# A two-block transformer kernel on one Trainium2 core: transposes and splits of the next linear's input inside the last chunk of the linear before

## The reference, cut to what matters

```python
# block 1
h = x + rms_norm(pool_mixer(rms_norm(x))) * post_gain      # pool_w_out: 4096 -> 2048
h = h + sigmoid(rms_norm(h) @ ple_w_gate) * (p @ ple_w_proj)
h = h + rms_norm(mla(rms_norm(h))) * post_gain              # mla_w_in, ..., mla_w_out
h = h + sigmoid(rms_norm(h) @ ple_w_gate) * (p @ ple_w_proj)
# block 2
mem_n = rms_norm(mem)
h = h + hybrid_mixer(rms_norm(h))                           # w_in: 2048 -> 6168, w_out
h = h + cross_attention(rms_norm(h), mem_n)                 # w_cq, w_ckv, w_co
h = h + conv_ffn(rms_norm(h))                               # w_up, w_down
out = rms_norm(h)
```

## Time and profile before

| what | value |
|---|---|
| median of 3 runs | 2591.68 us (2591.64 to 2591.83) |
| the profiled execution, its own time | 2595.02 us |
| its span in the trace | 2593.2 us |
| PE busy | 2519.5 us, 97% of the span |
| DVE busy | 1540.7 us, 59% |
| ACT busy | 1326.6 us, 51% |
| POOL busy | 83.7 us, 3% |
| mean granted TensorE clock | 0.995 of full speed |
| read from memory | 447.25 MB, 173 GB/s over the span |

### The profile page before, as it was taken

How to read it: one execution, slowest core, us unless ns; L and a number is a source line. 1 busy time by engine, 2 the same in 40 slices (tenths; PEclk the granted TensorE clock), 3 DMA queues, 4 the chain that set the end, 5 groups by cost and what they waited for, 6 DMA issues and landing times. The chain is left out here.

```text
span 2593.2 us, 34914 instructions
## 1 busy us (share of the span) xinstructions
PE 2519.5 (97%) x12890; PEld 2140.7 (83%) x12890; DVE 1540.7 (59%) x1814; ACT 1326.6 (51%) x1747; POOL 83.7 (3%) x124
## 2 busy tenths in 40 slices
PE   8999999999999999999899998899999999999998
PEld 7888888888778898778688887777888888888886
DVE  6665766644655555565555445755666666776554
ACT  5544444544656656464555445435544544554443
POOL 0000000000000000110100002000000000000010
PEclk9999999999999999999999999999999999999999
DMA  8666666555455543565566662054456666656563
GB/s 294 189 188 189 186 188 185 200 194 185 163 162 182 176 132 132 179 228 187 155 181 182 190 190 64 30 165 146 130 172 192 180 193 182 190 171 202 195 199 110
DMA packets 233424, 450.95 MB, mean 174 GB/s; under 512 B 14468, under 2 KB 59728, under 8 KB 232285
## 3 DMA queue, kind: packets, MB, share of 16 engines
q1 hardware_dynamic: 230518, 435.97, 54.2%
q0 software_dynamic: 2624, 13.27, 1.5%
q10 hardware_dynamic: 168, 0.19, 0.0%
HBM read 447.25 MB, written 2.12 MB: 173 GB/s over the span
## 5 line engine op out<-in xcount | busy, mean ns | idle before, releaser
L1598 DVE TENSOR_TENSOR w_lo<-raw,w_hi 128x1024 fp32r<-128x1024 f32 x852 | 1047.2, 1234 | 820.6 <-ACT w_hi L1102 801.6
L1102 ACT ACTIVATE w_hi<-raw 128x1024 fp32r<-128x1024 f32 x852 | 898.9, 1059 | 995.1 <-PE ps L648 637.0
L669 PE MATMUL ps<-x_hi_lo,w_hi 128*128 128x512 f32 x2336 | 822.9, 394 | 13.9 <-DVE w_lo L1598 13.9
L671 PE MATMUL ps<-x_hi_lo,w_lo 128*128 128x256 f32 x2336 | 661.1, 283 | 0.0
L669 PEld LDWEIGHTS ps<-x_hi_lo,w_hi 128*128 128x128 f32 x2336 | 439.4, 188 | 117.0 <-issue 8.7
L646 PE MATMUL ps<-w_hi,x_hi_lo 128*128 128x512 f32 (+3 forms) x1280 | 500.9, 391 | 21.1 <-DVE x_hi_lo L1627 12.4
L648 PE MATMUL ps<-w_hi,x_hi_lo 128*128 128x512 f32 (+3 forms) x1280 | 493.1, 385 | 0.0
L647 PE MATMUL ps<-w_lo,x_hi_lo 128*128 128x512 f32 (+3 forms) x1280 | 491.5, 384 | 0.0
L671 PEld LDWEIGHTS ps<-x_hi_lo,w_lo 128*128 128x128 f32 x2336 | 439.8, 188 | 0.0
L646 PEld LDWEIGHTS ps<-w_hi,x_hi_lo 128*128 128x128 f32 x1280 | 241.5, 189 | 76.3 <-issue 23.8
L648 PEld LDWEIGHTS ps<-w_hi,x_hi_lo 128*128 128x128 f32 x1280 | 241.2, 188 | 43.2
(11 more groups left out here) (316 smaller groups left out, 2200.4 us busy)
## 6 DMA issues: line engine op xcount, KB each, us to landing
raw<-in_w_up SPq DMA_DIRECT2D x160, 512.0 KB, 3.9
raw<-in_pool_w_in SPq DMA_DIRECT2D x128, 512.0 KB, 3.8
raw<-in_w_in SPq DMA_DIRECT2D x96, 480.0 KB, 4.0
raw<-in_w_down SPq DMA_DIRECT2D x76, 512.0 KB, 4.6
raw<-in_pool_w_out SPq DMA_DIRECT2D x64, 512.0 KB, 4.4
raw<-in_ple_w_gate SPq DMA_DIRECT2D x64, 512.0 KB, 4.0
raw<-in_mla_w_in SPq DMA_DIRECT2D x56, 448.0 KB, 3.5
raw<-in_pool_w_group SPq DMA_DIRECT2D x32, 512.0 KB, 4.3
```

What stands on the lines that cost most here:

```text
L669: pe.matmul(bank, w_hi[:, slot, cols], xs[:, k].rearrange("p s n -> p (s n)"), start=k == 0, stop=False, skip_group_check=True)
L671: last = pe.matmul(bank[:, 0:T], w_lo[:, slot, cols], xs[:, k, 0, :], start=False, stop=k == nkt - 1, skip_group_check=True)
L1102: act.activation(w_hi[:, u % RING, :], raw[:, slot, :], ACT.Copy).then_inc(S("w_hi"), 1)
L1598: dve.tensor_tensor(w_lo[:, u % RING, :], raw[:, u % RAW, :], w_hi[:, u % RING, :].bitcast(F32), ALU.subtract)\
```

## The change

PE gets `turn` and `early_turns` as functions of their own. `early` is the number of groups that a first chunk finds already done. On PE turn g of the next linear stands ahead of unit g + 1 of the last chunk in front of it, so that tile pair g of the old input has been read when group g is overwritten:

```diff
-        def first_chunk(src, source_ready=None, width=512, banks_ready=None, run=chunk):
+        def first_chunk(src, source_ready=None, width=512, banks_ready=None, run=chunk, early=0):
-            first = t.n["bank"]
+            first = t.n["bank"] - early
             def ready(k):
                 if k % 2 == 0:
-                    if k // 2 + 3 < KT // 2:
-                        turn(k // 2 + 3)
+                    if early <= k // 2 + 3 < KT // 2:
+                        turn(src, source_ready, k // 2 + 3)
                     n = first + k // 2
                     pe.wait_ge(S(f"t_free{n % 4}"), n // 4 + 2)
-            for g in range(3):
-                turn(g)
+            for g in range(early, 3):
+                turn(src, source_ready, g)
+        def early_turns(src, source_ready, n):
+            def ready(k):
+                if k % 2 == 0 and 2 <= k <= 2 * n:
+                    turn(src, source_ready, k // 2 - 1)
+            return ready
```

The two gates get 2 early groups, turned between the third and the fourth chunk of the projection; `mla_in`, `z`, `cq` get 6 in the last chunk in front of them:

```diff
-        def layer_end(n, ready_ple):
+        def layer_end(n, ready_ple, last):
+            updated = lambda g: pe.wait_ge(S(f"h_post{n}"), g // 2 + 1)
             for c in range(NCH):
                 chunk(ph, pl, 2, ready=ready_ple if c == 0 else None)
...
+                if c == 2:
...
+                    for g in range(2):
+                        turn(h, updated, g)
+            linear(h, updated, early=2, last=last)
...
-        first_chunk(h, lambda g: gated(pe, 0, g // 2 + 1), MIN_W)
+        updated0 = lambda g: gated(pe, 0, g // 2 + 1)
+        layer_end(0, ready_ple, early_turns(h, updated0, 6))
+        first_chunk(h, updated0, MIN_W, early=6)
```

For `z` the matmul of the position table (line 971), its waits and ACT's copy of it move from behind both `ckv` chunks to between them. For `up`, whose linear in front has four short chunks, two turns and groups follow each of the chunks 1 to 3 of `co`, and the `co` input moves to the last four tiles of x, which groups 6 and 7 alone overwrite:

```diff
         for c in range(NCH):
-            chunk(xh, xl, 4, ready=ready if c == 0 else None)
+            chunk(xh[:, 12:16], xl[:, 12:16], 4, ready=ready if c == 0 else None)
+            if c:
+                for g in (2 * c - 2, 2 * c - 1):
+                    turn(h, lambda g: chunk_out(pe, "co", g // 2), g)
```

ACT and DVE follow. In ACT's last chunk a group now includes its square and stands ahead of a unit; in the first chunk after it six units come ahead of group 6:

```diff
+        def early_groups(n, *args, ready=None, **kw):
+            hi(2)
+            for g in range(n):
+                if ready:
+                    ready(g)
+                group(g, *args, **kw)
+                hi(1)
+            hi(6 - n)
...
             for g in range(KT // 2):
-                if features is None:
...
+                if g >= early:
+                    if ready:
+                        ready(g)
+                    group(g, g0, src, slot, features)
                 hi(1)
```

DVE has the same without squares. Its `layer_end` splits groups 0 and 1 after the second of the three plain chunks of the projection; `update(2)` and `update(3)` stay in the gate's first chunk. For `ckv`, ACT waits before group g until PE has used unit g of the gate's last chunk (`gate1_units`); nothing is turned there. The loads of the memory move forward on POOL:

```diff
             for c in range(NCH):
                 chunk_out(pool, ("pool_out", "mla_out")[n], c)
+                if n == 1 and c == 0:
+                    load(memf, a["mem_features"], "mem_in")
+                    load(memt, tokens(a["mem_2"][0]), "mem_in")
...
-        load(memf, a["mem_features"], "mem_in")
-        load(memt, tokens(a["mem_2"][0]), "mem_in")
         gated(pool, 1)
```

More of the change, by code:

```diff
@@ L723, in first_chunk, with turn, linear @@
             run(xh, xl, KT, width, ready)
[L725 to L729, removed]
+        def turn(src, source_ready, g):
+            if source_ready:
+                source_ready(g)
+            to_bank(src, g * 256)
+        def early_turns(src, source_ready, n):
[3 more added lines that the diff above has]
+            return ready
+        def linear(src, source_ready=None, banks_ready=None, early=0, last=None):
+            first_chunk(src, source_ready, banks_ready=banks_ready, early=early)
+            for c in range(3):
+                chunk(xh, xl, KT, ready=last if c == 2 else None)
         def columns(xhi=xh, xlo=xl, nkt=KT, turns=2, ready=None, width=512):
@@ L1285, in layer_end @@
                 read_out(chunk(1), lambda tt: proj[:, tt, c * 512:(c + 1) * 512])
+                if c == 2:
+                    for g in range(2):
+                        group(g, GAIN[f"ple{n}"], h, slot + 1)
             for c in range(NCH):
-                s = first_chunk(GAIN[f"ple{n}"], h, slot + 1) if c == 0 else chunk(8)
+                s = first_chunk(GAIN[f"ple{n}"], h, slot + 1, early=2) if c == 0 else chunk(8) if c < 3 else chunk_with(next_groups)
                 act.wait_ge(S("gated"), 4 * n + c + 1)
@@ L1434, in _, with gate1_units, memory_groups @@
                 split_p(1)
[L1435 to L1440, removed]
+        def gate1_units(g):
+            products(act, "gate1", g - 7)
+        def memory_groups():
+            act.wait_ge(S("mem_in"), 32)
+            early_groups(6, GAIN["mem"], memt, 8, memf, ready=gate1_units)
+        layer_end(1, 6, memory_groups)
+        s = first_chunk(GAIN["mem"], memt, 8, features=memf, early=6, ready=gate1_units)
+        read_out(s, lambda tt: kvm[:, tt, 0:512], scale=8)
         from_bank(relrow, (slice(0, A_H), slice(0, 384)))
@@ L1631, in xpose_lo, with group, early_groups, first_chunk @@
                 t.add("xh")
-        def first_chunk(g0=None, slot=None, between=None, features=None, sem=None):
-            for g in range(KT // 2):
[L1636 to L1640, removed]
+        def group(g, g0=None, features=None, sem=None):
+            k = slice(2 * g, 2 * g + 2)
+            if features is None:
+                xpose_lo(xl[:, k, :], xh[:, k, :], 2, None if g0 is None else g0 + 2 * g)
+            else:
+                split_lo(xl, xh, features, g, g0, sem)
+        def early_groups(n, *args):
+            lo(2)
+            for g in range(n):
+                group(g, *args)
+                lo(1)
+            lo(6 - n)
+        def first_chunk(g0=None, slot=None, between=None, features=None, sem=None, early=0):
+            for g in range(KT // 2):
+                if g >= early:
+                    group(g, g0, features, sem)
                 lo(1)
@@ L1871, in layer_end @@
             update(1)
-            for c in range(3):
+            for c in range(2):
                 skip(1)
-            first_chunk(GAIN[f"ple{n}"], slot + 1, lambda g: update(g + 2) if g < 2 else None)
+            for g in range(2):
+                group(g, GAIN[f"ple{n}"])
+            skip(1)
+            first_chunk(GAIN[f"ple{n}"], slot + 1, lambda g: update(g + 2) if g < 2 else None, early=2)
             evacuated(dve, f"proj{n}")
```

103 lines of the change are left out of this document (59 added, 44 removed).

## The result

The changed kernel takes 2577.09 us as the median of 4 runs (2576.34 to 2577.79); the kernel before, on the same chip, 2591.76 (2591.64 to 2593.82). The ratio is 0.9939, with a 95% interval of 0.9926 to 0.9951: 14.7 us faster, where 16.7 and a time of 2575.0 were forecast; the range of 2570.5 to 2581.0 holds it. The profiled execution took 2577.78 on its own clock.

What follows compares the result with a forecast made beforehand. PE, 97% busy, bounds the kernel; its waits for x's low part in first chunks can go. Savings 1.35 + 1.2 + 2.6 + 3.4 + 8.2 + 0 = 16.7 us, from the median 2591.7 to 2575.0; range 2570.5 to 2581.0.

Steps and rivals of the forecast that it cites:

- The mechanism: First chunks: early turns and groups remove PE's waits for x's low part, 16.7 us saved in all; chance 0.60.
- half moved: Rival, last chunks: early groups make PE wait some 0.3 us at each of 24 turns, 2582 us; chance 0.10.
- The rival of ACT and DVE falling behind: Last chunks, 30 units with early groups: ACT and DVE run one after the other, 2613 us; chance 0.02.
- Unit 6's wait: First chunks with six early groups: group 6 queues behind six w_hi and w_lo; a 0.93 us wait stays in cq.
- The loop of 3.7 us: First chunks: PE's end of unit g through w_hi, w_lo and x's low part to unit g + 2; a unit lasts 2.78.
- h's late end: mla_in: h's last chunk ends 7.4 us after PE's end, costing 0.1 at turn 6 and 0.3 at unit 7.
- The gates: 0: Both gates: start wait exchanged for 2.0 us before unit 1; 0 net, between 1.5 saved and 1.2 lost each.
- the slow clock behind the gates' start: Rival and wrong sign: the gates' new wait lowers the clock, 1.7 us at each gate, 2578.4 us; chance 0.15.
- within 0.2 of before: Gates: after unit 1's wait, update(3) and the groups catch up, so unit 2 starts within 0.2 us of before.
- the term for the clock: ckv's start: PE near 1.2 GHz after idling loses 1.7 us, counted within the 8.2 us saved there.
- ckv's wait was for a late transfer: Rival, ckv's start: tokens still come late, so 3.25 us and the clock's 1.7 stay, 2580.0 us; chance 0.05.
- the loop at unit 6 does not hold PE: Rival: no wait at unit 6, and the gates save what their waits allow, 2567 us; better than forecast, chance 0.06.

Runs made afterwards that it cites:

- the second trace of the kernel before: The kernel before profiled once more, no edit: 2592.93 us, ratio 0.9998; its trace is 2.24 us shorter than the forecast's.
- the second trace: The changed kernel run and profiled once more, no edit: 2576.71 us, ratio 0.9937 to the kernel before.
- two reorderings: Changed kernel without early groups at the gates but update(2), update(3) moved into the projection: 2577.76 us; groups alone 2576.71, neither 2575.62, both 2569.87.
- ordering ACT's and DVE's queues around them: Changed kernel plus update(2), update(3) moved into the projection and groups one unit earlier in every first chunk: 2560.60 us, ratio 0.9879.

## Why the forecast was right, and where not

**The mechanism held.** All five places with six early groups saved what was worked out or a little more: 3.84, 8.43, 2.84, 1.55 and 1.50 us, 18.2 in all, against 3.4 + 8.2 + 2.6 + 1.35 + 1.2 = 16.7. The turns cost 0.46 each in the last chunks (3.23 us from one to the next, 3.24 forecast), so nothing was half moved. The rival of ACT and DVE falling behind did not show either. Unit 6's wait is there too, each time 0.2 shorter than its term: 1.06 for 1.27 in mla_in, 0.72 for 0.93 in ckv, 0.92 for 1.09 in z, 0.71 for 0.93 in cq, 0.67 for 0.85 in up. Its cause is shown by its going when the group was taken earlier.

**Too small by 1.5 us in these five.** Unit 6's wait is 0.2 under its term at each of the five, 1.0 in all. The loop of 3.7 us was read where the square stood on ACT between `w_hi` and the group, and DVE's split, which needs the group's high part, began 1.34 us behind its `w_lo` (1797.05 and 1798.39 in the earlier trace rows); in front of unit 6 no square stands there, and the split follows after 1.15 (1245.64 and 1246.79). In mla_in I had put aside 0.1 and 0.3 for h's late end. Its stretch has no wait beside unit 6's, so these terms were not needed. The two make 1.4. The edit that I did not price, the square's place, is worth 0.9 here (0.28 + 0.2 + 0.2 + 0.15 + 0.1), but not of these 1.5: with the square behind `w_hi` unit 7 waits as well, and the forecast had no wait there. It came true at unit 7 only by that unpriced edit.

**One small cost was not foreseen.** After cq, attention's first transpose waits 1.77 us where it waited 1.40, and the stretch is 0.35 longer with the change. ACT and DVE at that place, before:

```profile
1799.24 1.06 ACT L1102 ACTIVATE w_hi<-raw 128x1024 fp32r<-128x1024 f32 x1 [0.89 <-PE ps L648]
...
1802.49 1.26 ACT L1170 ACTIVATE cross_q<-ps,rstd 128x512 f32<-128x512 f32 x2 [0.41 <-PE ps L648]
```

and after:

```profile
1783.71 1.06 ACT L1118 ACTIVATE w_hi<-raw 128x1024 fp32r<-128x1024 f32 x1 [1.17 <-PE ps L648]
...
1786.83 1.27 ACT L1208 ACTIVATE cross_q<-ps,rstd 128x512 f32<-128x512 f32 x2 [0.29 <-DVE rstd L1721]
...
1784.80 1.23 DVE L1649 TENSOR_TENSOR w_lo<-raw,w_hi 128x1024 fp32r<-128x1024 f32 x1 [1.55 <-ACT w_hi L1118]
1785.94 0.15 DVE L1716 TENSOR_REDUCE mean_square<-square_sums 128x2 f32<-128x8 f32 x1
```

Before, PE's unit 7 had waited, so that ACT's `w_hi` began 0.17 us ahead of it (1799.24, 1799.41). Now it begins 0.26 behind unit 7 (1783.45 in PE's timeline), and the sum of squares, which stands behind the `w_lo`, comes as much later. The reading of cq used to wait for PE and now waits for `rstd`. This is read from the traces, and one more run agrees: with the square behind `w_hi` again the `w_hi` begins only 0.13 behind unit 7 (1786.65 and 1786.78), the wait is 1.59 and the stretch 0.19 longer than before. No run was made to try it.

**The gates: 0 was near in the first trace by luck.** The wait of 2.0 us in front of unit 1 was forecast and measured at 2.04 and 2.03, and unit 1 at 661.98 lies where 662.3 less the 0.3 us by which this launch started sooner puts it. But the slow clock behind the gates' start, which the prediction named as a sign of being wrong, came, and with it that rival: at one gate of two in one execution, and at both in the next. Both gates together stand at +0.09 and +1.68, for a forecast of 0. A fall costs 1.6 us (+0.86 against -0.77), where I had 1.7. I gave it 0.15 as a matter of yes or no; it is a chance for each wait and each execution. The lower stretch of -0.77 is that of a gate whose clock held. It gains 0.45 from the square, whose place shortens the gaps in front of units 5 to 7 to 0.29 to 0.36, where the forecast left them at 0.42; the other 0.3 stand at unit 2, which starts earlier by that much, where "within 0.2 of before" was forecast.

**ckv: the term for the clock may be an accident too.** In the earlier trace rows the clock fell behind 3.25 us of idle time; behind the same 3.25 us with the groups taken out again it stayed at 1.00. In the second trace of the kernel before it fell again, to 0.61, and of the kernel with ckv's groups late there is one trace only, so that chance is likely here but not shown. So 8.2 mixes about 6.5 that is saved in any case with 1.7 that is saved only against executions in which the clock fell. The Trainium skill, in TensorE: Matmul & The Clock Gate (Part 1), ties the clock to how busy the array was; here the same wait is followed by a fall and by none, so that by this case's traces the rule tells where a fall can come, not that it will.

**The step that was off is the one from the sum to the median.** The forecast took 16.7 from the first median of before, 2591.68 in 3 runs; every later median of that kernel, of 9 to 15 runs, is 2592.93 to 2593.7, so the level was some 1.4 too low. By spans the result is 17.2 against 16.7; between the first medians it is 14.7; with more runs of both kernels 16.4 (2593.09 - 2576.71). The miss of 2.1 us is of the size of such chance: the first 20 us (-0.1 to -1.1), mla_out's start (-1.0 or +1.3) and the gates (-0.8 or +0.9) move by 1 to 2 us each from one execution to the next, which is also the size of the steps within one kernel's runs (2576.34 and 2577.79). That the total came so near is in part luck as well: 1.5 us saved unforeseen in the five places stand against 0.35 lost behind cq and, in the second trace, 1.7 at the gates.

**The other rivals.** That ckv's wait was for a late transfer is refuted by the wait's staying with the early loads and by its not coming with the late ones. That the loop at unit 6 does not hold PE is refuted as well. The loads of the memory cost and bring nothing, as forecast.

## What to carry to other kernels

When a producer's stream feeds both the weights of the present unit and the input of a later one, put the input's part in front of the weights, one unit earlier than it is wanted: here moving transposes and splits into the chunk before brought 16 us, half of it at ckv, where nothing is turned, and ordering ACT's and DVE's queues around them 16 more, of which 1.7 may be the clock's, with no work added. An edit that takes a wait away is finished only when the engine that ended the wait has been read through: at the gates either of two reorderings alone gave nothing, both 5.8 us. Sum stretch by stretch between the same instructions of two traces, look at the granted clock in stretches that no edit touches, and take a second profile of each kernel before a difference of 1 to 3 us is believed.

## What the hardware showed that was not expected

- The same idle time of PE, in the same place of the same instructions, is followed by a granted clock near 0.6 in one execution and of 1.00 in the next: 2.03 us at the second gate (1.00, then 0.65), mla_out's start, with waits of 0.5 to 0.9 us (0.68, then 1.00), 2.1 us in out2's first chunk (0.63 in the kernel before, 1.00 without early groups at the gates), and 3.25 us in front of ckv (0.55 in the kernel before, 1.00 with ckv's groups late). A fall costs 1.6 us at a gate and up to 2.35 at mla_out's start.
- The first 20 us vary by 1 us between executions (-0.13 to -1.12 against the first trace of the kernel before).
- The stretches of mla_in, ckv, z, cq and up agree to 0.1 us between traces of kernels that are alike there, so that the 0.2 to 0.45 us of the square's place could be read from traces, where the medians of runs could not tell them.
